# Recurrence of a hybrid decoder layer: an own tile for the off-diagonal blocks, other operand roles for the sample queries, other PSUM banks, and part of the elementwise work on another engine

## Chip, core and metric

The kernel runs on one core of a Trainium2 chip. A core has TensorE (PE, with its weight loads as PEld), VectorE (DVE), ScalarE (ACT), GpSimd (POOL) and the queue engine SyncE (SP), all with their own instruction streams that wait for one another by semaphores. The metric is the device time of one launch in microseconds; lower is better.

## What is computed

The launch runs two layers of a decoder trunk in float32, for a prompt of 512 tokens and 8 samples of 8 tokens, 576 columns in all. Each layer has a pooling mixer, a gated linear recurrence (HGRN2), latent attention, their merge, and a gated feed-forward part. The change touches the recurrence and, through the engine that prepares it, the pooling mixer. Per head (4 heads, key and value size 128) the recurrence is:

```python
def step(S, blk):
    qc, kc, vc, lc = blk
    L = jnp.cumsum(lc, axis=2)
    inter = jnp.einsum('bhtk,bhkv->bhtv', qc * jnp.exp(L), S)
    diff = jnp.where(causal, L[:, :, :, None, :] - L[:, :, None, :, :], -jnp.inf)
    A = jnp.einsum('bhtk,bhsk,bhtsk->bhts', qc, kc, jnp.exp(diff))
    intra = jnp.einsum('bhts,bhsv->bhtv', A, vc)
    L_end = L[:, :, -1:, :]
    S = jnp.exp(L_end[:, :, 0, :, None]) * S + jnp.einsum('bhsk,bhsv->bhkv', kc * jnp.exp(L_end - L), vc)
    return S, inter + intra
```

The pooling mixer has 4 groups of 128 channels with windows 2, 4, 8 and 16; a group's mean minus the token goes through a 128x128 matrix.

## The kernel before

Tokens lie along the free dimension, channels along the 128 partitions. Every engine's order is written out by hand; there is no scheduler. A layer runs: input projections, attention, sample attention, then the stretch of this study, then the merge quads, output, feed-forward.

**The stretch before the recurrence.** PE projects the pooling input (four tiles `TILE_U`), the gate (four tiles `TILE_HGATE`) and then the four pooling products (`TILE_YPOOL`), which wait for `pool_d_ready`. Meanwhile POOL works out, for heads 0 and 1, the exponents of seven levels (`level_differences`, line 646) and of the ends (`ends_differences`, line 665), ACT takes their exponentials (`decays_levels`, `decays_ends`), and POOL multiplies by the queries (`level_scaled`, line 657, and `ends_scaled`). DVE does the pooling mixer.

**The recurrence.** There are 20 steps `n`: for each head, 4 chunks of 128 prompt tokens and one sample step (`c == 4`) of 64 columns. PE runs `hg_pair_scores(n+1)` ahead of `hg_sums(n)`. A pair part has 28 matmuls of 32-column weights (lines 1044, 1048 and 1053: diagonal blocks in an even bank, off-diagonal ones in an odd bank) and a transposition of the keys (line 1058) into bank 6. DVE masks and sums the levels and writes the diagonal blocks into `scores_hg` (lines 2235, 2238, 2244: `pair_sums`); ACT copies the keys out of bank 6 and then, behind `hg_scores`, three off-diagonal blocks into the same `scores_hg` (line 1558, `hg_full`). The sums part has scores times values (line 1068), queries times state (line 1073) and keys times values (line 1078), after which DVE updates the state (line 2261: `update`). In a sample step PE multiplies the 8 states as weights of 128 columns by 8 query columns each (line 1090) and the keys by the values laid out in 8 blocks, two matmuls of 512 columns over 64 partitions (line 1098), into bank 7 and into the odd bank of that step; DVE then updates 8 states (line 2273). The pair part two steps on writes that odd bank and waits for `hg_state`.

**Heads 2 and 3** are prepared inside the recurrence: POOL takes the differences and `ends_scaled`; ACT takes the exponentials at the steps that `LEVEL_STEPS` and `END_STEPS` name (step: head, first level, end); DVE does `level_scaled` behind steps 4 and 13. POOL's differences of head 3 come behind `ends_scaled` of head 2, and its buffers are free when head 0's or head 1's sample step is done (`hg_upd`). After the last step PE sums squares (line 880 from `lq`, `ones`) and starts the merge.

## Time and profile before

| | us |
|---|---|
| median of 3 runs (lowest, highest) | 2368.7 (2366.51, 2369.54) |
| the profiled execution, its span | 2366.31, 2364.5 |
| PE busy in the span | 2258.8 (96%) |
| DVE, ACT, POOL busy | 1167.7, 507.0, 1085.3 |
| recurrence, first layer (first pair matmul to first square sum) | 324.98 to 398.85 |
| recurrence, second layer (first pair matmul) | from 1497.02 |

The span is the profiled time between the first and the last instruction; 1.8 us of the execution lie around it. The granted clock is the share of TensorE's full 2.4 GHz that it was given; 0.50 is 1.2 GHz.

### The profile page before, as it was taken

How to read it: one execution, taken by the hardware profiler on the slowest of the kernel's cores; microseconds unless marked ns; L12 is line 12 of the kernel's file. 1: busy time of each engine (PE TensorE's matmuls, PEld its weight loads, DVE VectorE, ACT ScalarE, POOL GpSimd, SP SyncE). 2: the span in 40 equal slices, each digit the busy share in tenths (PEclk: the TensorE clock that was granted, in tenths of full speed). 3: DMA queues.
4: the chain of work that ended last, by engine and by line, in shares of the span. 5: the costliest groups of instructions: out<-in, count | busy, mean ns of one | idle time of the engine just before them, and what ended most of it. 6: DMA issues, size and time to landing. Idle time of an engine off the chain costs nothing.

```text
span 2364.5 us, 36665 instructions
## 1 busy us (share of the span) xinstructions
PE 2258.8 (96%) x11752; PEld 1734.4 (73%) x11752; DVE 1167.7 (49%) x1983; ACT 507.0 (21%) x1066; POOL 1085.3 (46%) x1260
## 2 busy tenths in 40 slices
PE   8999888999998999999899989889999899999997
PEld 6775676777776777777676757667777677777775
DVE  0534464432466666671216345553325766666612
ACT  1434334111112001000124333331111211001002
POOL 0000545666664676633300007446666646676342
PEclk9999997999999999999999999879999999999998
DMA  5221121222212222222032221222221312222211
GB/s 205 91 81 49 56 77 65 81 80 73 72 68 107 71 82 78 71 81 74 36 128 85 72 62 41 78 73 73 81 81 63 120 57 86 71 79 75 81 62 40
DMA packets 51612, 183.42 MB, mean 78 GB/s; under 512 B 7234, under 2 KB 27970, under 8 KB 37762
## 3 DMA queue, kind: packets, MB, share of 16 engines
q1 hardware_dynamic: 50882, 178.49, 22.0%
q10 hardware_dynamic: 576, 3.00, 0.3%
q8 instruction: 82, 1.34, 0.2%
q14 instruction: 72, 0.59, 0.1%
HBM read 172.28 MB, written 9.18 MB: 77 GB/s over the span
## 4 chain that ended last, share of the span: by engine, by line
PE 86%; DVE 4%; SPq 4%; issue 3%; POOL 1%; ACT 1%; DMA 0%; DVEq 0%; ACTq 0%; POOLq 0%
PE ps L1177 24%; PE ps L1105 19%; PE ps L1215 16%; PE ps L880 14%; PE ps L1453 3%; PE ps L1380 2%; PE ps L901 2%; SPq L717 1%; SPq L729 1%; PE ps L1245 1%; SPq L722 1%; PE ps L912 1%; PE ps L1098 1%; DVE xT L2006 1%; PE ps L1367 1%
## 5 line engine op out<-in xcount | busy, mean ns | idle before, releaser
L880 PE MATMUL ps<-xT,wring 128*128 128x288 f32 (+2 forms) x1152 | 280.5, 406 | 1.4 <-DVE o_mla L2176 1.4
L880 PEld LDWEIGHTS ps<-xT,wring 128*128 128x128 f32 x1152 | 218.7, 190 | 62.0 <-issue 1.7
L1177 PE MATMUL ps<-lq,mreg 128*128 128x288 f32 x1008 | 251.3, 406 | 0.0
L1177 PEld LDWEIGHTS ps<-lq,mreg 128*128 128x128 f32 x1008 | 191.5, 190 | 52.9
L1558 ACT ACTIVATE r<-ps 128x288 f32<-128x288 f32 (+7 forms) x268 | 113.1, 428 | 537.1 <-PE ps L1105 251.7
L1177 PE MATMUL ps<-xT,wring 128*128 128x288 f32 x672 | 169.8, 406 | 0.0
L1177 PEld LDWEIGHTS ps<-xT,wring 128*128 128x128 f32 x672 | 127.7, 190 | 35.3
L1105 PE MATMUL ps<-r,kbuf 128*128 128x288 f32 x576 | 143.6, 406 | 0.0
L2636 POOL TENSOR_TENSOR kbuf<-o_mla 128x288 f32<-128x288 f32 x42 | 33.3, 794 | 221.9 <-DVE o_mla L2406 221.9
L653 POOL TENSOR_TENSOR side<-lq 128x256 f32<-128x256 f32 x20 | 13.0, 652 | 258.7 <-PE ps L1481 258.7
L1105 PEld LDWEIGHTS ps<-r,kbuf 128*128 128x128 f32 x576 | 109.4, 190 | 30.2
L2663 POOL TENSOR_TENSOR kbuf<-kbuf,lq 128x2304 f32<-128x2304 f32 x2 | 10.1, 5049 | 257.3 <-DVE side L2113 257.3
L1851 ACT ACTIVATE r<-r 128x592 f32<-128x592 f32 x44 | 30.7, 697 | 428.0 <-DVE r L2443 427.8
L1558 ACT ACTIVATE o_mla<-ps 128x288 f32<-128x288 f32 (+1 forms) x108 | 45.5, 421 | 338.4 <-PE ps L1215 214.5
L2443 DVE SCALAR_TENSOR_TENSOR r<-r,small 128x592 f32<-128x592 f32 x88 | 104.6, 1189 | 12.4 <-DVE r L2440 12.1
L2440 DVE SCALAR_TENSOR_TENSOR r<-r,small 128x592 f32<-128x592 f32 x88 | 104.5, 1188 | 12.4 <-DVE r L2437 11.4
L1105 PE MATMUL ps<-xT,wring 128*128 128x288 f32 x384 | 97.2, 407 | 1.8 <-ACT lq L1580 1.8
L1215 PE MATMUL ps<-r,side 128*128 128x288 f32 x372 | 92.7, 407 | 0.8 <-DVE r L2454 0.8
L1105 PEld LDWEIGHTS ps<-xT,wring 128*128 128x128 f32 x384 | 72.8, 190 | 22.7 <-issue 2.7
L1177 PE MATMUL ps<-xT,mreg 128*128 128x288 f32 x336 | 88.3, 406 | 0.0
L1177 PE MATMUL ps<-lq,wring 128*128 128x288 f32 x336 | 88.3, 406 | 0.0
L1105 PE MATMUL ps<-lq,r 128*128 128x288 f32 x336 | 87.6, 407 | 0.7 <-DVE side L2324 0.7
(412 smaller groups left out, 4595.9 us busy)
## 6 DMA issues: line engine op xcount, KB each, us to landing
wring<-w_stream SPq DMA_DIRECT2D x100, 1024.0 KB, 4.9
side<-w_stream SPq DMA_DIRECT2D x18, 704.0 KB, 4.3
r<-pages_in SPq DMA_DIRECT2D x80, 128.0 KB, 2.1
vbuf<-w_stream SPq DMA_DIRECT2D x12, 512.0 KB, 3.7
r<-w_stream SPq DMA_DIRECT2D x12, 512.0 KB, 3.6
wring<-w_stream SPq DMA_DIRECT2D x8, 704.0 KB, 4.2
r<-w_stream SPq DMA_DIRECT2D x6, 704.0 KB, 4.2
mreg<-pages_in SPq DMA_DIRECT2D x32, 128.0 KB, 2.1
```

Source lines behind the costliest of these rows:

```text
L880: mm = pe.matmul(out[0:w.shape[-1], a * 512:a * 512 + hi - lo], w, x[:, lo:hi], start=(k == 0), stop=(k == len(pairs) - 1))
L901: mm = pe.matmul(slot(tile + j)[:, a * 512:a * 512 + hi - lo], w, xT[:, k, lo:hi], start=(k == 0), stop=(k == KD - 1))
L1105: mm = pe.matmul(banks[name], ws[:, k * P:(k + 1) * P], xs[:, k, :], start=(k == 0), stop=(k == n - 1))
L1177: mm = pe.matmul(up_sum[name], ws[:, k * P:(k + 1) * P], xs[:, k, :], start=(k == 0), stop=(k == HK - 1))
L1215: mm = pe.matmul(res_bank(which, m, i - 1), ws[:, k * P:(k + 1) * P], x, start=(k == 0), stop=(k == len(xs) - 1))
L1380: mm = pe.matmul(bank[2 * x + a][:, 0:HALF], w, xT[:, k, a * HALF:(a + 1) * HALF], start=(k == 0), stop=(k == KD - 1))
L1453: mm = pe.matmul(slot(TILE_HI + m)[0:rows, part * 256:(part + 1) * 256], xT[:, k, m * P:m * P + rows], w_slot[part][:, k * 256:(k + 1) * 256],
L1558: return act.activation(out, in_, func, **more)
L1851: act.activation(conv_h[u][0][:, 0:CX - 2], conv_h[u][0][:, 0:CX - 2], ACT.Silu).then_inc(silu_done.sem, 1)
L2440: dve.scalar_tensor_tensor(out=out, in0=src[:, 1:CX - 1], scalar=scalar(col + 2 * KF), in1=out, op0=ALU.mult, op1=ALU.add).then_inc(conv_s ...
L2443: dve.scalar_tensor_tensor(out=out, in0=src[:, 2:CX], scalar=scalar(col + 4 * KF), in1=out, op0=ALU.mult, op1=ALU.add).then_inc(conv_done. ...
L2636: pool.tensor_tensor(up_v[u], up_u2[u], up_p5s[u], ALU.add).then_inc(up_v_ready.sem, 1)
```

## The change

It does six things. (1) The off-diagonal blocks get a tile of their own, `off_hg`, zeroed once; ACT fills it as soon as the pair part is there, before the keys, and PE multiplies it by the values in a matmul of its own, ahead of the one with `scores_hg`. (2) In a sample step a 32-column window of queries is the weight and the state of each sample the moving operand; the rows go through `s_rows` and come back by two matmuls with a selecting matrix `pick`. (3) The keys times values of samples are two matmuls over 32 partitions each, in banks 7 and 6; the transposed keys move into the odd bank of the step. Waits of the pair part go. (4) DVE prepares heads 0 and 1 instead of POOL. (5) The pooling groups run in the order 3, 2, 1, 0. (6) `LEVEL_STEPS`, `END_STEPS` and the multiplication steps move.

```diff
-LEVEL_STEPS = {0: (2, 0, 2), 1: (2, 2, 5), 2: (2, 5, 7), 10: (3, 0, 2), 11: (3, 2, 5), 12: (3, 5, 7)}
-END_STEPS = {7: 2, 13: 3}
+LEVEL_STEPS = {3: (2, 0, 3), 5: (2, 3, 7), 10: (3, 0, 3), 11: (3, 3, 7)}
+END_STEPS = {7: 2, 12: 3}
+MULT_STEPS = {7: 2, 13: 3}
+GROUP_OF = (3, 2, 1, 0)
...
-            return bank[7] if part == 0 else bank[2 * (n % 2) + 1]
+            return bank[7 - part]
+
+        def turned_bank(n):
+
+            return bank[2 * (n % 2) + 1][:, P:2 * P]
...
-                if n >= 2 and (n - 2) % (N_CHUNK + 1) == N_CHUNK:
-
-                    pe.wait_ge(*hg_state.at(l, ((n - 2) // (N_CHUNK + 1) + 1) * (N_CHUNK + 2)))
-                if c == N_CHUNK:
-                    pe.wait_ge(*hg_k_rows.at(l, n))
...
-                if 1 <= n and c < N_CHUNK:
-                    pe.wait_ge(*hg_k_rows.at(l, n))
-                pe.transpose(bank[6][0:w, 0:P], decayed[:, h % 2, 1, t0:t0 + w], ident).then_inc(hg_turned.sem, 1)
+                pe.transpose(turned_bank(n)[0:w, :], decayed[:, h % 2, 1, t0:t0 + w], ident).then_inc(hg_turned.sem, 1)
...
-                    mm = pe.matmul(bank[4][:, t0:t1], v_hg[:, c, h * P:(h + 1) * P], scores_hg[:, n % 2, :],
-                                   start=True, stop=(c == 0))
+                    pe.matmul(bank[4][:, t0:t1], v, off_hg[:, n % 2, :], start=True, stop=False)
+                    pe.wait_ge(*hg_scores.at(l, n + 1))
+                    mm = pe.matmul(bank[4][:, t0:t1], v, scores_hg[:, n % 2, :], start=False, stop=(c == 0))
...
+                for b in range(DEC_BATCH):
+                    x, j = divmod(b, S_PAIRS)
+                    t0 = SEQ + min(DEC_SEQ * b, SAMPLES - SUB)
+                    mm = pe.matmul(bank[5][SUB * j:SUB * (j + 1), 256 + x * P:256 + (x + 1) * P],
+                                   decayed[:, h % 2, 0, t0:t0 + SUB], state_s[:, b, h, :], start=True, stop=True)
+                mm.then_inc(s_rows_made.sem, 1)
+                pe.wait_ge(*hg_k_rows.at(l, n + 1))
+                pe.wait_ge(*blocks_ready.at(l, h + 1))
+                pe.wait_ge(*hg_state.at(l, ups))
+                for part in range(2):
+                    rows = slice(SUB * part, SUB * (part + 1))
+                    pe.matmul(upd_bank(n, part), k_rows[rows, n % 2, :], v_blocks[rows, :, :],
+                              start=True, stop=True).then_inc(hg_upd.sem, 1)
+                pe.wait_ge(*hg_scores.at(l, n + 1))
+                pe.wait_ge(*hg_o_taken.at(l, 3 * h + 2))
...
+                for x in range(2):
+                    mm = pe.matmul(bank[5][:, 0:SAMPLES], s_rows[:, x * P:(x + 1) * P], pick[x], start=False,
+                                   stop=(x == 1))
...
-                pe.wait_ge(*taken_at(l, TILE_YPOOL + 1))
+                pe.wait_ge(*taken_at(l, TILE_YPOOL + 3))
...
+                def ready_head(h):
+                    dve.wait_ge(*lev_exp.at(l, h + 1))
+                    level_scaled(dve, h)
+                    dve.wait_ge(*ends_exp.at(l, h + 1))
+                    dve.tensor_tensor(decayed[:, h % 2, 0, :], decayed[:, h % 2, 0, :], q_hg[:, h, :], ALU.mult
+                                      ).then_inc(lev_ready.sem, 1)
+
+                dve.wait_ge(*smp_cols_taken.at(l, S_PAIRS))
+                dve.wait_ge(*log_k_ready.at(l, 1))
+                for h in range(2):
+                    level_differences(dve, h).then_inc(lev_diff.sem, 1)
+                    ends_differences(dve, h).then_inc(lev_diff.sem, 1)
...
+                    if i in (0, 2):
+                        ready_head(i // 2)
...
-                        dve.wait_ge(*hg_o.at(l, 2 * h + 2))
-                        dve.tensor_copy(q_hg[:, h, SEQ:T], bank[5][:, 0:SAMPLES]).then_inc(hg_o_taken.sem, 1)
+                        dve.wait_ge(*s_rows_made.at(l, h + 1))
+                        dve.tensor_copy(s_rows, bank[5][:, 256:512]).then_inc(hg_o_taken.sem, 1)
```

On PE, at the first sample step (step 4, behind the pair part of step 5), the program before has:

```order
L1058 MATMUL ps<-const,mreg 128x128 [waits hg_k_rows]
L1086 MATMUL ps<-mreg,vbuf 128x64 [waits state_s_ready,hg_scores]
L1090 MATMUL ps<-mreg,r 128x8 x8
L1097 REGISTER_ALU [waits blocks_ready,hg_k_rows]
L1098 MATMUL ps<-mreg 128x512 [waits hg_state]
L1098 MATMUL ps<-mreg 128x512
L1031 REGISTER_ALU [waits hg_scores]
L1044 MATMUL ps<-lq,r 32x32 [waits hg_state]
```

The changed program has at the same place:

```order
L1062 MATMUL ps<-const,mreg 128x128
L1093 MATMUL ps<-r1,mreg 32x128 [waits state_s_ready]
L1093 MATMUL ps<-r1,mreg 32x128 x7
L1096 REGISTER_ALU
L1098 REGISTER_ALU [waits blocks_ready,hg_k_rows]
L1101 MATMUL ps<-mreg 128x512 [waits hg_state]
L1101 MATMUL ps<-mreg 128x512
L1104 ISA [waits hg_scores]
L1105 MATMUL ps<-mreg,vbuf 128x64 [waits hg_o_taken]
L1108 MATMUL ps<-const,r2 128x64 x2
L1050 MATMUL ps<-lq,r1 32x32 [waits hg_scores]
```

The scores matmul moved behind the state updates and now waits for DVE's copy of the rows; the wait of the next pair part for DVE's state updates is gone.

On PE, in a chunk step, the changed program has one matmul more (L1073 with `off_hg`), and the wait for the scores stands behind it:

```order
L1062 MATMUL ps<-const,mreg 128x128
L1073 MATMUL ps<-off_hg,vbuf 128x128 [waits hg_full]
L1074 REGISTER_ALU
L1075 MATMUL ps<-mreg,vbuf 128x128 [waits hg_scores]
L1077 REGISTER_ALU
L1079 MATMUL ps<-mreg,side 128x128 [waits hg_state]
L1084 MATMUL ps<-vbuf,mreg 128x128 [waits hg_k_rows]
```

On DVE, ahead of the pooling mixer (the last instructions of head 1's differences, then the first sums of pooling group 3), the changed program has:

```order
L665 TENSOR_TENSOR r<-kbuf,lq 128x4x64
L678 TENSOR_TENSOR r<-kbuf,lq 128x576
L680 TENSOR_TENSOR mreg<-lq,kbuf 128x64
L2213 REGISTER_ALU
L2219 TENSOR_TENSOR r<-r 128x710 [waits tile_act]
```

Behind that group come head 0's multiplications:

```order
L2230 SCALAR_TENSOR_TENSOR r<-r 128x496
L2236 SCALAR_TENSOR_TENSOR r<-r 128x64
L2239 COPY r<-r 128x15
L2240 COPY r<-r 128x120
L673 TENSOR_TENSOR side<-side,lq 128x256 [waits lev_exp]
L673 TENSOR_TENSOR mreg<-mreg,lq 128x32
```

Before, DVE went from the copies of the history (L2183) straight to the first group's sums (L2196); the differences and multiplications of both heads stood on POOL.

## Rows read from the trace of the kernel before

**Rows 1.** The page, busy time by engine.
```profile
PE 2258.8 (96%) x11752; PEld 1734.4 (73%) x11752; DVE 1167.7 (49%) x1983; ACT 507.0 (21%) x1066; POOL 1085.3 (46%) x1260
```

**Rows 2.** Windows over both recurrences: engines busy, granted clock, DMA share, GB/s.
```profile
324.98:398.85 73.87, 58.06 (x1158) 44.78 (x1157) 44.60 (x137) 31.09 (x103) 35.79 (x37) 0.78 0.17 63
1497.02:1572.00 74.98, 61.65 (x1158) 46.83 (x1158) 44.65 (x137) 31.33 (x103) 36.83 (x37) 0.72 0.16 62
```

**Rows 3.** Timeline, PE, sample step of head 0 at the full clock: start, us.
```profile
335.92 0.27 PE L1044 MATMUL ps<-lq,r 128*32 128x32 f32 x8
336.87 0.43 PE L1086 MATMUL ps<-mreg,vbuf 64*128 64x64 f32 x2
337.23 1.95 PE L1090 MATMUL ps<-mreg,r 128*128 128x8 f32 x16
339.12 1.98 PE L1098 MATMUL ps<-mreg 64*128 64x512 f32 x4
343.07 0.34 PE L1044 MATMUL ps<-lq,r 128*32 128x32 f32 x8 [1.98 <-DVE r L2273]
```

**Rows 4.** Timeline, PE, the sums of a chunk at the full clock.
```profile
390.15 0.39 PE L1068 MATMUL ps<-mreg,vbuf 128*128 128x128 f32 x2
390.37 0.39 PE L1073 MATMUL ps<-mreg,side 128*128 128x128 f32 x2
390.91 0.26 PE L1044 MATMUL ps<-lq,r 128*32 128x32 f32 x4
```

**Rows 5.** Timeline, PE, head 3 at 1.2 GHz, then the square sums.
```profile
374.89 0.69 PE L1086 MATMUL ps<-mreg,vbuf 64*128 64x64 f32 x2
379.02 3.78 PE L1098 MATMUL ps<-mreg 64*128 64x512 f32 x4
386.37 0.34 PE L1044 MATMUL ps<-lq,r 128*32 128x32 f32 x8
389.16 0.34 PE L1044 MATMUL ps<-lq,r 128*32 128x32 f32 x8
398.85 6.29 PE L880 MATMUL ps<-lq,ones 128*128 128x288 f32 x16 [1.22 <-DVE r L2273]
```

**Rows 6.** Timeline, PE, matmuls over 32 partitions in the sample attention.
```profile
219.49 1.09 PE L970 MATMUL ps<-r,side 32*64 32x512 f32 x8
```

**Rows 7.** Timeline, DVE, level sums of a chunk and state updates of samples.
```profile
332.33 0.36 DVE L2235 TENSOR_TENSOR r<-ps,const 128x192 f32<-128x192 f32 x1 [0.35 <-PE ps L1053]
333.26 0.29 DVE L2244 TENSOR_TENSOR mreg<-ps,const 128x128 f32<-128x128 f32 x1
357.18 2.16 DVE L2273 SCALAR_TENSOR_TENSOR r<-r,end_decay,ps 128x128 f32<-128x128 f32 x8 [0.83 <-PE ps L1098]
```

**Rows 8.** Timeline, the preparation of head 3 on ACT and POOL.
```profile
348.43 0.68 ACT L1759 ACTIVATE r<-r 128x576 f32<-128x576 f32 x1
352.43 0.61 POOL L653 TENSOR_TENSOR side<-lq 128x256 f32<-128x256 f32 x1
362.59 1.41 POOL L667 TENSOR_TENSOR r<-kbuf,lq 128x576 f32<-128x576 f32 x1
369.27 0.68 ACT L1759 ACTIVATE r<-r 128x576 f32<-128x576 f32 x1
373.39 0.34 PE L1044 MATMUL ps<-lq,r 128*32 128x32 f32 x8 [3.07 <-POOL mreg L2530]
```

**Rows 9.** Timeline, the stretch ahead: pooling on DVE, the products on PE.
```profile
276.03 6.61 DVE L2196 TENSOR_TENSOR r<-r 128x710 f32<-128x710 f32 x1 [15.04 <-ACT r L1558]
309.20 0.21 DVE L2217 COPY r<-r 128x120 f32<-128x120 f32 x1
320.99 4.06 PE L880 MATMUL ps<-r,small 128*128 128x288 f32 x16
```

**Rows 10.** Timeline, DVE, multiplications of a head's levels.
```profile
369.34 0.42 DVE L662 TENSOR_TENSOR side<-side,lq 128x256 f32<-128x256 f32 x1
369.68 0.18 DVE L662 TENSOR_TENSOR mreg<-mreg,lq 128x32 f32<-128x32 f32 x1
```

134 lines of the change are left out of this document (60 added, 74 removed).

## The prediction

> **What bounds the kernel now.** I read the page by engine first: PE is busy 96% of the span [rows 1]. A change elsewhere is worth something only where PE waits, or runs slowly. The windows over the recurrences show both [rows 2]: in the first, 73.87 us long, PE is busy 58.06 us, so it waits 15.8; in the second, 74.98 us to its end mark, 61.65. And the granted clock is 0.78 and 0.72, a mixture of 2.4 and 1.2 GHz with some 44% and 56% of the time at the lower. No other engine is near full there (DVE 44.6 us). The timeline then shows what ends PE's waits. Behind the sample step of head 0, PE stands 1.98 us until DVE has updated the sample states [rows 3]; before head 3 it stands 3.07 us for POOL's last product [rows 8].
>
> **A chunk step on PE.** At the full clock pairs and transposition take 336.87 - 335.92 = 0.95 us [rows 3] and the sums 390.91 - 390.15 = 0.76, so 1.71 together; one matmul of the sums is 390.37 - 390.15 = 0.22 [rows 4]. The change adds one (`off_hg` times values): 1.93. At 1.2 GHz the same step is 389.16 - 386.37 = 2.79 [rows 5], and the added matmul 0.43 (twice 0.22): 3.22. So on 16 chunk steps a layer the edit costs PE 3.5 us at the full and 6.9 at the half clock. What it buys: the sums part need not wait for ACT's copies behind the scores. DVE's chain from mask to scores is 333.26 + 0.29 - 332.33 = 1.22 us [rows 7], and it lies beside 1.93 us of PE; then nothing on the path waits for ACT in a plain step.
>
> **A sample step on PE.** Now, from the start of the 64x64 matmul to the end of the updates: 339.12 + 1.98 - 336.87 = 4.23 us at the full clock [rows 3], and 379.02 + 3.78 - 374.89 = 7.91 at the half [rows 5]. After it:
> - 8 matmuls with 32-column weights and 128 moving columns, 16 passes. A pass of 128 columns is 0.11 us (half of the 0.22 [rows 4]). Four column groups side by side, as the pair parts use them, give 16 x 0.11 / 4 = 0.44; two side by side 0.88; one after the other 1.76. I take 0.44, since 48 passes of pair work and a transposition fit into 0.95 us [rows 3].
> - two updates of 512 columns over 32 partitions, in two banks. One after the other they cost today's 1.98 us [rows 3]; side by side half. The nearest row is the sample attention's, 8 passes of 512 columns over 32 partitions in 1.09 us [rows 6], where one by one they would need 8 x 1.98 / 4 = 3.96. I take 1.0.
> - scores and two selecting matmuls of 64 columns, with two new full weight loads: 0.5.
>
> Sum 1.95 us at the full clock, 3.8 at the half: 2.3 to 4.1 us less for each of 8 sample steps, and 1.3 to 3.2 even if nothing runs side by side in the updates.
>
> **The wait behind it** changes place. The next pair part starts at once, but the next head's first update writes bank 7 and waits for DVE's 8 state updates (2.16 us [rows 7]), which now have a copy of 256 columns, some 0.4 us, ahead. PE has 0.5 + 0.95 + 0.66 us of other work for this, so I leave 0.6 us of waiting where 1.98 stood [rows 3]. Queued behind that waiting matmul is all of PE; DVE waits in turn only for that update.
>
> **The stretch before.** The pair part now waits for all four pooling products to be taken: +0.9 us. DVE gets, for each of two heads, 14 large and 6 small differences, two more for the ends, and 7 + 3 + 1 products. With 0.34 us for a large (369.68 - 369.34) and 0.18 for a small one [rows 10], and 0.7 for one of 576 columns: some 6.9 and 4.0 us a head. The 13.8 us of differences fill the 15.04 us in which DVE waits for ACT [rows 9]; the 8.0 of products lie ahead of the pooling's end, which is 309.20 + 0.21 = 309.4, while PE first needs it at 320.99 [rows 9]. 11.6 us of cover, so this costs nothing; without the cover it would cost up to 8 a layer. The other order of groups is hidden by the same cover. POOL, freed, begins head 2's differences earlier, which hides them deeper.
>
> **The first seven steps.** I count PE's work until the transposition of step 7 is ready and ACT can begin head 2's end exponentials: seven pair parts of 0.95, one sample pair of 0.6, four sums 3.9, one sample step 1.95, two sums 2.0, waits 0.9, the late start 0.9, ACT's copies 0.65. That is 16.9 + 0.6 from 324.98, so 342.5; before it was 348.43 [rows 8]. **5.9 us**.
>
> **From there to head 3** another chain sets the time: ACT's ends of head 2, POOL's product, POOL's differences of head 3 (362.59 - 352.43 = 10.2 us), ACT's exponentials and ends, POOL's product. It took 373.39 - 348.43 = 25.0 us [rows 8]. The change touches one link: exponentials in two pieces instead of three and the ends a step earlier, 5.6 by the same rows instead of 369.27 - 362.59 = 6.7 [rows 8]. PE would be through its five to six steps sooner, so it waits: here part of the gain is given back as waits for ACT, on the first sums of head 2. Head 3 begins at 342.5 + 23.9 = 366.4, **7.0 us** earlier in all.
>
> **Head 3** took 398.85 - 373.39 = 25.5 us [rows 5, 8], much of it at 1.2 GHz. After, at the full clock: five pair parts 4.4, two sample steps 3.9, sums 3.8, and waits 3.0 (last one: 2.16 of updates and a copy behind the selecting matmuls): 15.1. All at the half clock: 27.2. Before, the clock fell behind waits and behind 8-column matmuls and rose during dense chunk steps. The 8-column matmuls go, the wait before head 3 stays. I take the middle, 21.1: **4.4 us**. The square sums behind it take 6.29 us, mostly at 1.2 GHz [rows 5]; 16 such matmuls take 4.06 at the full clock [rows 9]. Half of the 2.2 between, **1.1 us**.
>
> The Trainium skill, "TensorE: Matmul & The Clock Gate" (Part 1: The HAM clock gate), says that the throttled state is the default and activity releases it. By that rule the denser sample step would keep the clock up, and head 3 would come nearer 15.1 than 21.1. The rows agree so far as dense steps stand before each rise; they don't say which head will be how dense.
>
> **Sum.** 7.0 + 4.4 + 1.1 = 12.5 us a layer, and 25 for two. The profiled execution took 2366.3 (span 2364.5 and 1.8 around it); the median of the three runs lies 2.4 above it. 2366.3 - 25 = 2341, and with part of that distance I say **2342 us**.
>
> **Rivals.**
> - *The clock stays up.* Without 8-column matmuls no stretch may be sparse enough. Then head 3 is 15.1 and the square sums 4.1: 7.0 + 10.4 + 2.2 = 19.6 a layer, 2327 to 2329. Against it: PE waits 3 us and more for ACT in head 2, and the clock fell behind less.
> - *Head 3 stays at 1.2 GHz and heads 0 and 1 lose clock as before.* Head 3 27.2, 2.5 us lost ahead of it: 7.0 - 2.5 - 1.7 = 2.8 a layer, 2361. For it: the added matmul costs most here, and the wait ahead of head 3 is still there.
> - *Slower: the lower clock throughout the recurrence.* Place: all 20 steps. 16 x 3.22 + 4 sample pairs of 1.1 + 4 x 3.8 + 5.3 of waits = 76.4 against 73.9 and 74.4: +4.5 for two layers, 2371. It decides when more than about nine tenths of PE's work is at 1.2 GHz, against 44% and 56% of the time now.
> - *DVE late for the pooling products.* Its added 21.8 us would have to cost more than about 33 to use up the cover. Operations of 256 columns at twice the 0.34 would cost some 10 us a layer on the path: 2361 again.
> - *Row tiles don't run side by side.* +1.0 x 8 at most, of which waits hide some: 2347. It lies in the forecast's own range.
>
> The Trainium skill, "TensorEngine Tiling (Array Packing)" (Tiling Modes, Key Properties), says that changing the tiling mode drains TensorE. That speaks against the sample step, which now goes through one or two more modes. No row isolates a drain; the pair-to-transposition change lies inside the 0.95 us above. The sum would rise by little, and no chance changes.
>
> **Numbers.** Forecast (2335 to 2352) 0.58, clock up 0.14, clock low in head 3 or DVE late 0.20, slower 0.05, no effect at all 0.03. To leave out no more than 2 in 10 the range goes from 2328 to 2359. This kernel's measurement can tell about 0.2%, or 4.7 us: faster 0.92, same 0.03, slower 0.05.
>
> **What would show it.** Sample steps of about 2 us at the full clock, the eight state matmuls in under 0.5, the two updates in about 1.0. No wait of the pair matmuls for DVE; instead the keys-times-values matmul of a head's first chunk waits for it. PE waits for ACT's copies in head 2's chunks, in all more than before. POOL's head 3 differences end near 356. The pooling products start at 321 as now. Wrong: if the first recurrence is over 68 us, look at the clock by head first; if it is under 56, at whether the chain over POOL bound at all.

## The result: 16 us faster, and the profile after

The changed kernel takes **2352.05 us** (median of 4 runs, 2350.25 to 2355.85) against 2368.12 for the kernel before in the same comparison (4 runs, 2366.51 to 2369.54). The ratio is 0.9934, with a 95% interval of 0.9917 to 0.9952: 16 us less, 12 to 20 by the interval. The forecast was 2342, with a range of 2328 to 2359. The profiled execution took 2352.96, its span is 2351.1. The page by engine, as in [rows 1]:

```profile
PE 2240.8 (95%) x11848; PEld 1719.8 (73%) x11848; DVE 1171.9 (50%) x2124; ACT 505.5 (21%) x1066; POOL 995.4 (42%) x1128
```

The windows over the two recurrences, from the first pair matmul to the first square sum, and over head 3 of the first layer (columns as in [rows 2]: length, busy time of the engines, granted clock, DMA share, GB/s):

```profile
329.19:392.13 62.94, 46.55 (x1205) 36.98 (x1205) 45.11 (x140) 28.45 (x102) 33.47 (x37) 0.95 0.20 74
1492.93:1559.33 66.40, 53.59 (x1205) 41.55 (x1205) 44.59 (x140) 28.57 (x102) 34.49 (x37) 0.82 0.19 70
374.86:392.13 17.27, 14.60 (x328) 11.22 (x328) 13.83 (x45) 4.08 (x19) 14.19 (x9) 0.90 0.01 2
```

The first recurrence went from 73.87 to 62.94 us. The second, which ended at 1571.38 before (1571.38 - 1497.02 = 74.36), went to 66.40. That is 10.9 and 8.0 us. Up to that same mark the second window of the kernel before reads:

```profile
1497.02:1571.38 74.36, 61.03 (x1158) 46.33 (x1157) 44.65 (x137) 31.33 (x103) 36.21 (x37) 0.72 0.17 62
```

All of this gain is in TensorE's busy time, which fell by 11.5 and 7.4 us (58.06 to 46.55, 61.03 to 53.59); part of that is less work, part the higher granted clock. TensorE is still busy only 46.55 of 62.94 us in the first, so 16.4 us of waiting are left, about as much as the 15.8 before, though the waits that I had read there are gone. The timeline of TensorE names the new ones; the steps in between are left out:

```profile
333.85 0.42 PE L1050 MATMUL ps<-side 128*32 128x32 f32 x26
336.45 0.29 PE L1050 MATMUL ps<-side 128*32 128x32 f32 x11 [2.19 <-issue]
...
340.42 0.63 PE L1093 MATMUL ps<-r,mreg 128*32 128x128 f32 x12
342.49 0.41 PE L1093 MATMUL ps<-r,mreg 128*32 128x128 f32 x4 [1.44 <-issue]
...
366.05 0.80 PE L1073 MATMUL ps<-off_hg,vbuf 128*128 128x128 f32 x2 [5.22 <-ACT off_hg L1568]
...
374.86 0.24 PE L1050 MATMUL ps<-lq,r 128*32 128x32 f32 x5 [1.31 <-issue]
```

Two things stand out. In the pair part of step 3, and inside the sample step of head 0, TensorE stops in the middle of a row of like matmuls (after 26 of 37, after 12 of 16) for 2.19 and 1.44 us, and the profile names no releaser. Layer 1 has the same two stops, at the same instructions, with 2.68 and 1.71 us. And at step 11 it waits 5.22 us for ScalarE's copy into `off_hg`. In layer 1, where TensorE came to these steps more slowly, that wait is spread over steps 10, 11 and 12 (1.43, 0.90 and 1.58 us). The stop at 374.86 is put down to issue as well, but it has a plain cause: VectorE's products of head 3, which this pair part waits for, end at 374.75 (its row is below).

The sample step of head 3, as in [rows 3], and the square sums, as in [rows 5]:

```profile
387.44 0.65 PE L1093 MATMUL ps<-r,mreg 128*32 128x128 f32 x16
388.44 1.13 PE L1101 MATMUL ps<-mreg 32*128 32x512 f32 x4 [0.36 <-DVE side L2286]
389.50 0.43 PE L1105 MATMUL ps<-mreg,vbuf 64*128 64x64 f32 x2
389.86 0.66 PE L1108 MATMUL ps<-const,r 128*128 128x64 f32 x4
392.13 5.81 PE L891 MATMUL ps<-lq,ones 128*128 128x288 f32 x16 [1.61 <-DVE lq L2304]
```

The states' 16 passes take 0.65 us (1.95 before), the updates 1.13 (1.98). The pair matmuls behind a sample step start at once, where they stood 1.98 us for VectorE [rows 3].

### The profile page after: what moved, and what is told of

It is laid out like the page before. It is cut to its first block, busy times and chain, and to the rows that moved or that the text cites. A ratio compares the mean times of both kernels' runs of the same rounds, so it can differ in the third digit from the quotient of the medians.

```text
span 2351.1 us, 36952 instructions
## 1 busy us (share of the span) xinstructions
PE 2240.8 (95%) x11848; PEld 1719.8 (73%) x11848; DVE 1171.9 (50%) x2124; ACT 505.5 (21%) x1066; POOL 995.4 (42%) x1128
## 4 chain that ended last, share of the span: by engine, by line
PE 86%; SPq 4%; DVE 4%; issue 3%; POOL 1%; ACT 1%; DMA 0%; DVEq 0%; ACTq 0%; POOLq 0%
PE ps L1188 24%; PE ps L1116 19%; PE ps L1226 16%; PE ps L891 14%; PE ps L1464 3%; PE ps L1391 2%; PE ps L912 2%; SPq L728 1%; SPq L740 1%; PE ps L1256 1%; SPq L733 1%; PE ps L923 1%; PE ps L1050 1%; DVE xT L2016 1%; PE ps L1378 1%
## 5 line engine op out<-in xcount | busy, mean ns | idle before, releaser
L2558 POOL TENSOR_TENSOR mreg<-vbuf,const 64x512 f32<-64x512 f32 x8 | 8.3, 1033 | 272.2 <-PE ps L1492 263.0
L2467 DVE SCALAR_TENSOR_TENSOR r<-r,small 128x592 f32<-128x592 f32 x88 | 104.6, 1189 | 12.4 <-DVE r L2464 10.9
```

Of the source, the lines that this page charges most:

```text
L2467: dve.scalar_tensor_tensor(out=out, in0=src[:, 1:CX - 1], scalar=scalar(col + 2 * KF), in1=out, op0=ALU.mult, op1=ALU.add).then_inc(conv_s ...
```

## Experiments

Every kernel was timed in turn with the kernel before on one chip; the medians of the kernel before in these comparisons lie between 2368.1 and 2369.8 us, and a step n means the same as above (steps 0 to 4 are head 0, 5 to 9 head 1, 10 to 14 head 2, 15 to 19 head 3). The columns are the median, its ratio to the kernel before with the 95% interval, and for the two layers of the profiled execution the length of the recurrence and the clock granted in it.

| kernel | us | ratio | layer 0 | layer 1 |
|---|---|---|---|---|
| before | 2368.1 | | 73.9 (0.78) | 74.4 (0.72) |
| changed | 2352.05 | 0.9934 (0.9917, 0.9952) | 62.9 (0.95) | 66.4 (0.82) |
| e1_loads_late | 2347.3 | 0.9914 (0.9901, 0.9927) | 62.8 (0.86) | 62.8 (0.84) |
| e2_loads_mid | 2353.2 | 0.9941 (0.9928, 0.9954) | 66.7 (0.85) | 64.5 (0.79) |
| e3_levels_first | 2360.1 | 0.9968 (0.9958, 0.9977) | 69.6 (0.85) | 69.4 (0.83) |
| e4_off_after_sums | 2352.95 | 0.9931 (0.9919, 0.9943) | 66.7 (0.85) | 68.0 (0.77) |
| e5_same_rows | 2357.6 | 0.9959 (0.9944, 0.9974) | 69.2 (0.78) | 69.6 (0.78) |
| e6_queries_moving | 2361.9 | 0.9971 (0.9959, 0.9983) | 71.1 (0.73) | 68.3 (0.82) |
| e7_gpsimd_prepares | 2353.0 | 0.9934 (0.9917, 0.9950) | 63.4 (0.95) | 62.8 (0.95) |
| e8_before_loads_late | 2368.3 | 0.9996 (0.9988, 1.0005) | 73.7 (0.75) | 74.5 (0.75) |
| e9_states_held | 2361.1 | 0.9965 (0.9954, 0.9976) | 69.8 (0.78) | 69.9 (0.80) |
| c1_split_differences | 2349.1 | 0.9918 (0.9904, 0.9931) | 64.7 (0.79) | 62.8 (0.81) |
| c2_port_in_turn | **2331.95** | 0.9847 (0.9834, 0.9859) | 54.3 (0.93) | 53.3 (0.97) |
| c3_in_turn_off_waits | 2329.9 | 0.9844 (0.9829, 0.9859) | 55.6 (1.00) | 55.4 (1.00) |

How far one profile can be trusted shows in e7_gpsimd_prepares: in the recurrence TensorE has the same instructions as in the changed kernel, and its second recurrence took 62.8 us at a granted clock of 0.95 where the changed kernel's took 66.4 at 0.82. A single recurrence is known to some 4 us. The intervals are 2 to 4 us wide on either side, so two kernels whose medians lie closer than that are not told apart.

### What the new stops are

The theory: they are TensorE's own instructions coming late. The trace has packets of 16 KB on an instruction queue (q8); it doesn't say for which engine. In the DMA view of the changed kernel for 334 to 335 us and for 340 to 340.5, one such packet moves inside the bulk transfers that are issued at 329 to 331 (2 MB of sample states, 0.27 MB of `pool_o`, twice 1 MB of `wring`):

```profile
q1 hardware_dynamic: 18, 0.29, 91.4%
q8 instruction: 1, 0.02, 6.0%
...
q1 hardware_dynamic: 29, 0.22, 104.8%
q8 instruction: 1, 0.02, 12.4%
```

TensorE stops at 334.3 and goes on at 336.45; it stops at 341.05 and goes on at 342.49. Later packets, with no transfer beside them (345 to 350, 350 to 355), have no stop. The packet itself takes about 1 us of one DMA engine in either case (6.0% of a microsecond of 16 engines here, 6.3% at 347), so if instructions come late, the time is lost around the packet and not in it. The rival: the stops belong to these places of the program. Two kernels move the transfers, with the same edit in SyncE's program, once with step 12 and once with step 5 as the mark.

```diff
+                sp.wait_ge(*hg_pairs.at(l, 13))
                 sp.dma_start(pool_out[bass.ds(l, 1)].rearrange("o p g n c -> (o p) g n c"), pool_last
                              ).then_inc(mixer_stored.sem, 16)
                 load(l, MERGE0)
                 load(l, MERGE0 + 1)
```

> The changed kernel with three transfers of the recurrence (the store of pool_o and the first two 1 MB loads of wring) held back until the pair part of step 12 is done; only the 2 MB load of the sample states stays where it was. Theory (the new idle times of TensorE put down to issue, 2.19 us at 336.45 and 1.44 us at 342.49 in layer 0, 2.68 and 1.71 in layer 1, are TensorE's own instructions arriving late, because a 16 KB packet of the instruction queue stands in line with the bulk transfers): the gap inside the sample step of head 0 is gone in both layers (1.4 + 1.7 = 3.1 us), the one in the pair part of step 3, which lies inside the load of the states, stays; about 2349 us. If the loads now meet another instruction packet, near step 13 to 16, a gap of 1 to 2 us shows up there instead and the time stays at 2352. Rival (the gaps belong to the place in the program, whatever the transfers do): both gaps stay, 2352 us.

> The same three transfers held back only until the pair part of step 5 is done, some 345 us into the execution. In the changed kernel an instruction packet moves between 345 and 350 and again between 350 and 355 with no transfer beside it and no gap on TensorE. Theory (instructions arrive late behind bulk transfers): the gap at 342.5 is gone, and a gap put down to issue of 1 to 2.5 us appears in steps 5 to 9 of head 1, where there was none; about 2352 us. Rival (gaps belong to the place in the program): the gaps stay where they were and none appears in head 1; 2352 us. The two differ in where the gaps are, not in the time.

TensorE's timeline of e1_loads_late, steps 3 and 4:

```profile
332.62 0.29 PE L1051 MATMUL ps<-side 128*32 128x32 f32 x11 [2.21 <-issue]
...
336.59 0.65 PE L1094 MATMUL ps<-r,mreg 128*32 128x128 f32 x16
```

The 16 passes of the states now run through in both layers; the stop in step 3 is where it was, under the load of the states. And of e2_loads_mid, in head 1 of layer 0, with the DMA view of 345 to 346 us:

```profile
347.46 0.22 PE L1051 MATMUL ps<-r 128*32 128x32 f32 x1 [2.32 <-issue]
```

```profile
q1 hardware_dynamic: 61, 0.39, 95.5%
q8 instruction: 1, 0.02, 6.0%
```

A stop of 2.32 us appeared in a pair part of head 1, where there had been none, with an instruction packet among the moved loads (at 345.3) 2 us ahead of its end. In layer 1 none appeared, and the time stayed. There the moved loads ran from 1508 to 1516, between two packets: the one at 1507.5 came ahead of them and the one at 1515.75 when they filled only 10% of the engines. So no packet met them in that layer, and both layers fit the theory. The third kernel holds the load of the states back too, until the pair part of step 3 is done.

```diff
                 sp.wait_ge(*taken_at(l, TILE_YPOOL + 3))
+                sp.wait_ge(*hg_pairs.at(l, 4))
                 sp.dma_start(state_s.rearrange("p b h v -> p (b h v)"),
```

> e1_loads_late with the 2 MB load of the sample states held back as well, until the pair part of step 3 is done, so that nothing bulky moves in the first three steps. Theory (the gap of 2.2 us in the pair part of step 3 is the same as the other: instructions behind the states' transfer): that gap is gone in both layers or falls under 0.7 us; in return the sample step of head 0 waits for the states, which land 9 us after their issue: 3.5 to 5.5 us; about 2350 to 2354 us. Rival (the gap at step 3 belongs to the place in the program): it stays at 1.8 us or more.

```profile
331.74 0.27 PE L1052 MATMUL ps<-lq,r 128*32 128x32 f32 x8
331.83 0.51 PE L1052 MATMUL ps<-side 128*32 128x32 f32 x38
...
340.86 1.08 PE L1095 MATMUL ps<-r,mreg 128*32 128x128 f32 x16 [4.76 <-DMA r<-hgrn_state]
```

The pair part of step 3 runs through, in both layers, and in its place stands the forecast wait for the states, 4.76 and 4.55 us. The packets at 333.0 and 1503.5 come about half a microsecond ahead of the load here, and no stop follows them. So each of the two stops goes when its transfer goes, and one came where a transfer was put: that bulk transfers cause the stops is shown. That what comes late is TensorE's instructions is inferred from the packets beside each stop. The time (2361) is 7 us above the expected range: besides the wait for the states, both recurrences ran at a clock of 0.78 and 0.80, for 0.86 and 0.84 in e1_loads_late; why they did is open. The Trainium skill, "Runtime: NRT & Kernel Launch" (Instruction fetch mechanics), says that instructions come in blocks of 16 KB over a queue of their own, and that the cost of a block's end is mostly hidden. The packets of 16 KB agree; where bulk transfers fill the engines, 1.4 to 2.7 us a block were not hidden here.

> The kernel before with the same three transfers held back until the pair part of step 12. Its trace has no gap put down to issue in either recurrence, though its instruction packets at 334 to 336 and 338 to 340 move inside the same transfers. Theory (TensorE ran slowly enough there, at half the clock for long stretches and with waits of 3 us in the first five steps, that its instructions came in time behind the transfers): no change, 2366 to 2371 us, so the 5 us that holding back gives the changed kernel were a cost that the change had brought. Rival (the transfers slow something else of the recurrence, the PSUM or SBUF side, in both kernels): 2364 us or less.

The kernel before gains nothing from the same edit (0.9996). One packet a layer moves well inside the transfers there (at 335.1 and 1508.3; the one at 338.75 comes when they are nearly over, at 9% of the engines), and no stop follows. So a packet among bulk transfers is not enough for a stop. The likely reason is the pace: behind the packet at 335.1 stands the old sample step, in which TensorE needed only 22 matmul records for the 4.2 us from 336.87 to 341.10 [rows 3]. No run tests this by itself.

What it is worth in time: 2347.3 against 2352.05, 4.7 us, in line with 3.1 us of stops, but the intervals of the two ratios overlap (0.9917 to 0.9927 lies in both), and layer 0's recurrence stayed at 62.8, at a lower granted clock (0.86 for 0.95). The gain in time is likely, not shown.

### What holds head 3 back

The wait of 5.22 us at step 11 has a chain behind it that the changed kernel's rows on GpSimd and ScalarE show. GpSimd waits 4.33 us for head 2's exponentials, takes their product, and only then makes head 3's differences; ScalarE stands 7.29 us for these with TensorE's copies queued behind:

```profile
351.08 2.26 POOL L2553 TENSOR_TENSOR mreg<-mreg,lq 128x576 f32<-128x576 f32 x1 [4.33 <-ACT mreg L1775]
353.30 0.61 POOL L664 TENSOR_TENSOR side<-lq 128x256 f32<-128x256 f32 x1
...
363.56 1.48 ACT L1759 ACTIVATE side<-side 128x1536 f32<-128x1536 f32 x1 [7.29 <-POOL mreg L665]
```

The first try changes the order of two calls.

```diff
                 value_blocks(l, 1)
-                ends_scaled(l, 2)
                 differences(l, 3)
+                ends_scaled(l, 2)
```

> The changed kernel with two calls on GpSimd changed in order: the level differences of head 3 ahead of the product that ends head 2's preparation. In the changed kernel GpSimd sits idle 4.33 us for ScalarE ahead of that product (351.08) and finishes head 3's differences at 363.5, while ScalarE sits idle 7.29 us for them and TensorE 5.22 us (366.05) for ScalarE's copies queued behind. Theory (this chain is what kept head 3 from its forecast start): the 5.22 us wait goes to under 1, about 0.4 us comes at the first pair part of head 2, ScalarE's exps of steps 11 and 12 leave 1 to 3 us of waits; net 3 to 4 us for each layer, about 2345 us. Rival (GpSimd is the bound of the recurrence in any order, and head 2's product is then late): the wait moves to the first pair part of head 2 with 3 us or more, 2351 to 2355 us.

It went the wrong way, to 2360.1, by neither mechanism. GpSimd was through with the differences at 358.5, 5 us earlier, and the wait for ScalarE at step 11 was gone. But TensorE waited 9.49 us (8.66 in layer 1) for VectorE's scores. VectorE's and GpSimd's timelines of that kernel:

```profile
350.61 1.05 DVE L673 TENSOR_TENSOR r<-r,lq 128x256 f32<-128x256 f32 x1
353.57 6.36 DVE L673 TENSOR_TENSOR mreg<-mreg,lq 128x32 f32<-128x32 f32 x1
359.85 1.86 DVE L673 TENSOR_TENSOR r<-r,lq 128x256 f32<-128x256 f32 x6
```

```profile
353.12 0.25 POOL L664 TENSOR_TENSOR mreg<-lq 128x32 f32<-128x32 f32 x1
...
358.49 1.39 POOL L2553 TENSOR_TENSOR mreg<-mreg,lq 128x576 f32<-128x576 f32 x1
```

A product of 128x32, which takes 0.18 us [rows 10], stood 6.36 us, to 359.93; GpSimd's row of back-to-back operations ended at 358.49 + 1.39 = 359.88. The three products ahead of it got in between GpSimd's operations, at 0.93 to 1.21 us each (the first is shown). Those of VectorE's operations that read PSUM kept their times beside GpSimd (0.36, 0.50 and 0.29 us at 349.1 to 350.3 there). The Trainium skill, "SBUF — State Buffer" (Who interferes with whom), has this: a VectorE instruction with two SBUF inputs contends with a GpSimd instruction that reads SBUF, and the second to come is blocked for the whole of the other. The trace agrees on which instructions meet. It differs in how long: the fourth product waited out not one GpSimd instruction but some ten. Why it did and the first three did not is open. The changed kernel had paid a little of it, at 372.03 (1.39 us for another 128x32), and its next products end at the 374.75 that released head 3:

```profile
372.03 1.39 DVE L673 TENSOR_TENSOR mreg<-mreg,lq 128x32 f32<-128x32 f32 x1
...
374.01 0.74 DVE L673 TENSOR_TENSOR mreg<-mreg,lq 128x256 f32<-128x256 f32 x2
```

So the two engines' instructions with two SBUF inputs are best laid out in turn, like users of one resource. Two kernels try that, both with the loads late. The first:

```diff
-LEVEL_STEPS = {3: (2, 0, 3), 5: (2, 3, 7), 10: (3, 0, 3), 11: (3, 3, 7)}
+LEVEL_STEPS = {3: (2, 0, 3), 5: (2, 3, 7), 9: (3, 0, 3), 10: (3, 3, 7)}
-MULT_STEPS = {7: 2, 13: 3}
+MULT_STEPS = {8: 2, 13: 3}
...
+                pool.wait_ge(*hg_pairs.at(l, N_CHUNK + 1))
+                level_differences(pool, 3, 0, 4)
                 pool.wait_ge(*hg_upd.at(l, N_CHUNK + 2))
                 ends(l, 2)
                 value_blocks(l, 1)
+                level_differences(pool, 3, 4).then_inc(lev_diff.sem, 1)
                 ends_scaled(l, 2)
-                differences(l, 3)
```

> The changed kernel with the transfers held back as in e1_loads_late, and GpSimd's differences for head 3 in two pieces: levels 0 to 3 as soon as the pair part of step 4 is done (head 0's level buffer is free then, 338.4 in the changed kernel) and not 4.33 us idle later, levels 4 to 6 behind head 2's ends, the product of head 2's preparation last; VectorE's seven products of head 2 one step later (8, not 7), and ScalarE's exps of head 3 in steps 9 and 10 (10 and 11 before). What e3_levels_first showed is kept out of the way: there one of VectorE's products (128x32, both inputs in SBUF) stood 6.36 us beside a row of GpSimd's operations, and ended with the row. Theory (the chain GpSimd to ScalarE is what keeps head 3 late, and the products wait only while GpSimd works): GpSimd is through with head 3's differences about 10 us earlier than at 363.5, the wait of 4 to 5 us at step 11 goes, 0.5 to 1.5 us comes back for the products in step 8 and for ScalarE's exps; 3 to 4 us in layer 0 and 2 to 3 in layer 1 below e1_loads_late's 2347: about 2341 us. Rival (VectorE's products meet GpSimd again and hold the sums): waits of 3 us or more in steps 8 and 9, 2347 to 2355 us.

```profile
347.42 3.57 DVE L673 TENSOR_TENSOR r<-r,lq 128x256 f32<-128x256 f32 x1
```

```profile
349.30 1.40 POOL L2554 TENSOR_TENSOR mreg<-mreg,lq 128x576 f32<-128x576 f32 x1
```

```profile
353.36 0.34 PE L1051 MATMUL ps<-lq,r 128*32 128x32 f32 x8 [4.15 <-DVE r L673]
```

The rival came out: the differences are done at 349.3, the wait at step 11 is gone, and VectorE's first product stood 3.57 us until GpSimd's last operation had ended (350.70; the product at 350.99). TensorE waited 4.15 us in each layer for it, and 2.3 and 2.1 us more ahead of head 3, and the time is that of e1_loads_late, within the error. The second kernel puts one wait between them, and moves the products of head 3 from step 13 to step 12:

```diff
-MULT_STEPS = {8: 2, 13: 3}
+MULT_STEPS = {7: 2, 12: 3}
...
                 value_blocks(l, 1)
+                pool.wait_ge(*late_ready.at(l, 1))
+                ends_scaled(l, 2)
                 level_differences(pool, 3, 4).then_inc(lev_diff.sem, 1)
-                ends_scaled(l, 2)
```

ScalarE's first exponentials of head 3 (levels 0 to 2) no longer wait for the end of the differences there, since these levels are in the first piece.

> The changed kernel with the transfers held back as in e1_loads_late and GpSimd's and VectorE's use of two SBUF inputs put in turn: GpSimd makes head 3's levels 0 to 3 right behind the pair part of step 4, then head 2's ends and value blocks, waits for VectorE's products of head 2 (step 7 again, 2.7 us), and only then does head 2's product and levels 4 to 6. ScalarE's exps of head 3 in steps 9 and 10, VectorE's products of head 3 in step 12 (13 before). In c1_split_differences a single product (128x256) took 3.57 us until GpSimd's row ended and TensorE waited 4.15 us for it. Theory (VectorE's instructions with two SBUF inputs stand still while GpSimd has work, and nothing else of the recurrence is left between 4 and 12): no product of head 2 above 0.5 us each, no wait of 4 us or more in steps 7 to 11 of layer 0 (e1_loads_late had 4.17 there), about 1 us of waits behind each set of products; recurrences of 58 to 61 us against 62.8 in e1_loads_late, 2339 to 2344 us. Rival (the sum of what VectorE, GpSimd and ScalarE have to do for the two late heads sets the time, the wait goes elsewhere in each order): recurrences of 62 to 64 us again and 2347 to 2350.

```profile
347.24 1.85 DVE L673 TENSOR_TENSOR r<-r,lq 128x256 f32<-128x256 f32 x6
```

```profile
349.26 1.41 POOL L2554 TENSOR_TENSOR mreg<-mreg,lq 128x576 f32<-128x576 f32 x1 [2.76 <-DVE r L673]
```

```profile
327.99:382.28 54.29, 46.66 (x1205) 36.82 (x1205) 44.04 (x140) 28.70 (x102) 31.74 (x35) 0.93 0.24 86
1481.83:1535.10 53.27, 45.28 (x1204) 35.58 (x1205) 43.85 (x140) 28.58 (x102) 31.98 (x36) 0.97 0.25 87
```

**2331.95 us**, 38 below the kernel before and 20 below the changed one: the products run at 0.31 us a piece, GpSimd waits 2.76 us for them, and in each layer one stop of 2.1 us (step 3, under the states) and no wait of over 2 us is left. This beats both kernels. It lies 7 us below the expected range: with head 3's products out of GpSimd's way its pair part has no wait either, and the clock was higher than in e1_loads_late (0.93 and 0.97 for 0.86 and 0.84).

How much of this is the order? Against c1_split_differences the two recurrences of the profiles are 10.4 and 9.5 us shorter. TensorE's waits shrank by 4.1 and 3.5 of that; the other 6.3 and 6.0 are busy time of the same instructions at a higher granted clock (0.93 and 0.97 for 0.79 and 0.81). That the two rose together is seen in this pair of runs, not explained. And c2 differs from c1 in three things, the wait, the earlier products and ScalarE's wait that went; none was tried alone.

### What each part of the change brought

Four kernels undo one part each in the changed kernel, and a fifth undoes the first of these parts in c2_port_in_turn. First the own tile: ScalarE waits again for the sums.

```diff
                     if c < N_CHUNK:
+                        act.wait_ge(*hg_scores.at(l, n + 1))
                         full, off = off_hg[:, n % 2, :], bank[2 * (n % 2) + 1]
```

> The changed kernel with one part undone: ScalarE waits again for VectorE's summed block (hg_scores) of a chunk before it copies the off-diagonal blocks, though they go to their own tile. Nothing is left out. VectorE needs about 1.2 us from the end of a pair part to the summed block and ScalarE 0.78 us behind it, 2.0 us, where TensorE is back at the sums of that chunk after some 1.9 us at the full clock. Theory (the own tile takes a wait away that matters only at the full clock): 0.1 to 0.5 us for each of the 16 chunk steps of a layer that run at the full clock, 2 to 6 us for each layer less what lies under ScalarE's and VectorE's other waits; 2355 to 2362 us. Rival (the wait is hidden, and the gain of the change came from the sample steps and the earlier preparation alone): 2351 to 2354 us.

> c2_port_in_turn with the edit of e4_off_after_sums on top: ScalarE again waits for VectorE's summed block before it copies the off-diagonal blocks to their own tile. In the changed kernel that wait moved nothing (2352.95 against 2352.05), though both its recurrences looked longer in the profile (66.7 and 68.0 us against 62.9 and 66.4). Theory (the own tile takes away a wait that stands in every chunk step, and was covered in the changed kernel by the chain of head 3; in c2_port_in_turn, 54.3 and 53.3 us, that chain is gone and the steps run at the full clock at 1.7 to 1.9 us): 0.1 to 0.3 us for each of 32 chunk steps and 1 us where ScalarE's exps stand behind it, 3 to 10 us in all, 2335 to 2342 us. Rival (the copies are early enough with the wait too, and the own tile brings nothing in either): 2330 to 2334 us.

2352.95 and 2329.9: nothing, in both settings. The windows over the recurrences of c3_in_turn_off_waits, under those of c2_port_in_turn above:

```profile
328.92:384.54 55.62, 44.31 (x1205) 34.63 (x1205) 44.56 (x140) 28.89 (x102) 31.57 (x36) 1.00 0.24 84
1483.24:1538.64 55.40, 44.31 (x1204) 34.63 (x1205) 44.58 (x140) 28.98 (x102) 31.70 (x36) 1.00 0.24 84
```

With the wait back, TensorE stands 7.0 us for ScalarE's copies into `off_hg` in layer 0, where it stood 1.0, twice 2.5 us of it beside VectorE's products. But it had the full clock throughout and was busy 44.31 us, not 46.66. The recurrences are only 1.3 and 2.1 us longer, and the medians differ by 2 the other way, within the error. Waits and clock went opposite ways here; what ties them is left open.

Next the updates in two row groups, of which the second takes the same rows as the first (this leaves the states of four samples wrong):

```diff
-                    rows = slice(SUB * part, SUB * (part + 1))
+                    rows = slice(0, SUB)
```

> The changed kernel in which the second of the two state updates of a sample step takes the same 32 rows of weights and values as the first (so the states of four of the eight samples come out from the wrong rows; the instructions are the same in number and size). Theory of the forecast (the two updates run side by side because they use different rows of the array, four passes in 1.13 us where one pass of 512 columns alone takes 0.21 us of columns at 2.4 GHz and two updates one behind the other 1.7): 0.7 us more in each of 8 sample steps, of which the next pair part follows at once, 4 to 6 us in all, 2355 to 2358 us. Rival (they are one behind the other already, or the time is hidden behind VectorE's updates): 2351 to 2353 us.

The four passes of the updates in the sample step of head 0, at the full clock, and of head 2, at half:

```profile
340.18 1.98 PE L1101 MATMUL ps<-mreg 32*128 32x512 f32 x4
377.18 3.78 PE L1101 MATMUL ps<-mreg 32*128 32x512 f32 x4
```

And the same passes in different rows at half the clock, in head 2 of layer 1 of the changed kernel:

```profile
1542.55 2.08 PE L1101 MATMUL ps<-mreg 32*128 32x512 f32 x4
```

1.98 us against 1.13 at the full clock, 3.78 against 2.08 at half: the updates do run side by side in different rows and not in the same. The time is 5.5 us longer, as expected, but the intervals of the two ratios overlap (0.9944 to 0.9952 lies in both).

The next kernel puts the old product of the states back:

```diff
-                for b in range(DEC_BATCH):
-                    x, j = divmod(b, S_PAIRS)
-                    t0 = SEQ + min(DEC_SEQ * b, SAMPLES - SUB)
-                    mm = pe.matmul(bank[5][SUB * j:SUB * (j + 1), 256 + x * P:256 + (x + 1) * P],
-                                   decayed[:, h % 2, 0, t0:t0 + SUB], state_s[:, b, h, :], start=True, stop=True)
...
+                for b in range(DEC_BATCH):
+                    t0 = SEQ + b * DEC_SEQ
+                    mm = pe.matmul(bank[5][:, b * DEC_SEQ:(b + 1) * DEC_SEQ], state_s[:, b, h, :],
+                                   decayed[:, h % 2, 0, t0:t0 + DEC_SEQ], start=False, stop=(b == DEC_BATCH - 1))
```

> The changed kernel with the product of states and sample queries put back as it was (eight products with a 128-column state as weights and 8 moving columns, added to the scores' product ahead of the updates; no s_rows and no picks); the updates stay in their two row groups and banks. Nothing is left out. Theory (this edit and the updates made the sample step 2.3 us shorter at the full clock and 4 at half): by the rows of before the products of the eight samples took some 1.9 us and the new way 1.0 (0.44 and half a microsecond of picks), and the wait for VectorE's scores comes back ahead of the updates, in all 1.5 to 2.5 us for each of 8 sample steps, more where the clock is low; 2363 to 2372 us. Rival (the sample step's length lies behind VectorE's and ScalarE's work in all but one or two steps): 2352 to 2358 us.

```profile
355.84 1.99 PE L1095 MATMUL ps<-mreg,r 128*128 128x8 f32 x16
```

2361.9, 1 us below the expected range: 9.9 us for the queries as weights. On TensorE at the full clock it is 1.99 us of states and 0.4 of scores against 0.65 and 0.95. That is 0.8 us for each of 8 sample steps, 6 in all. The rest goes with the granted clock, 0.73 and 0.82 for 0.95 and 0.82, and with a longer last wait for VectorE's updates (2.2 us ahead of the square sums for 1.6).

The last part is the preparation of heads 0 and 1, given back to GpSimd:

```diff
-                for h in range(2):
-                    level_differences(dve, h).then_inc(lev_diff.sem, 1)
-                    ends_differences(dve, h).then_inc(lev_diff.sem, 1)
...
+                differences(l, 0)
+                ends(l, 0)
+                differences(l, 1)
+                ends(l, 1)
+                scaled(l, 0)
+                ends_scaled(l, 0)
                 value_blocks(l, 0)
+                scaled(l, 1)
+                ends_scaled(l, 1)
```

> The changed kernel with heads 0 and 1 prepared by GpSimd again (differences, ends and both products), VectorE having only the pooling; the order of ScalarE's exps and of the groups stays that of the changed kernel. Nothing is left out. Theory (this edit costs and brings nothing by itself: GpSimd was through with both heads at 304.5 in the kernel before and idle for 4.75 us and 21.7 us behind it, so head 2's differences are no later): 2350 to 2354 us. Rival (VectorE's pooling windows, which have both inputs in SBUF, stand still beside GpSimd's operations as its products did in e3_levels_first, and the pooling products come late): the first pair part starts 3 us or more later in its layer, 2357 us or more.

2353.0: the edit is worth nothing that the intervals could tell, as forecast. VectorE's cover held (in the changed kernel the pooling products wait for nothing of it), and GpSimd had nothing better to do.

So undoing the states' product costs some 10 us and undoing the row groups of the updates some 5.5, the latter within overlapping intervals; undoing the other two parts costs nothing. These are costs of single parts in the changed kernel, and it is chance that they add up to its 16 us. The other banks were not undone in any run, and with them the waits that the pair part lost: in the kernel before TensorE stood for VectorE behind a sample step (1.98 us [rows 3]), and in the steps of head 0 for ScalarE's copies of the keys, which had to leave bank 6:

```profile
330.28 0.33 PE L1058 MATMUL ps<-const,mreg 128*128 128x128 f32 x1 [1.26 <-ACT mreg L1558]
334.65 0.26 PE L1044 MATMUL ps<-lq,r 128*32 128x32 f32 x4 [0.89 <-ACT mreg L1558]
```

All of these are gone in the changed kernel. What that is worth in time stays open, and so does the order of ScalarE's exponentials and of the pooling groups, which was not tried alone either.

## The prediction, point by point

The forecast said faster, by 25 us, and it was 16. Its steps:

- **The chunk step** was forecast at 1.93 us at the full clock; the transpositions of steps 7 and 8 are 349.21 - 347.31 = 1.90 us apart. Right. That nothing on the path waits for ScalarE in a plain step was right too, but what the own tile was said to buy was nothing, by e4 and c3.
- **The sample step** was forecast at 1.95. The states take 0.6 (0.44 forecast), the updates 1.06 (1.0), but the scores and the two selecting matmuls 0.36 + 0.59 = 0.95 (0.5): 2.6 in all. This term was 0.65 us too small, 2.6 us a layer. The rival in which row tiles don't run side by side is excluded by e5.
- **The wait behind it**, 0.6 in place of 1.98: there is none behind the sample step; 0.4 to 0.6 us stand ahead of its own updates or scores. Right in size; I had put them ahead of the next head's first update.
- **The stretch before** was costed at nothing and 0.9 of a later start. The 0.91 us is there in every profile of the changed kernel and its variants, and the cover held: TensorE has no wait in its projections up to the last pooling product. That layer 0 began at 329.19 and not 325.9 is, as far as the traces tell, not the change: the long row of projections ahead of it already began 3.2 us later (262.04 for 258.81), and the profiles of the twelve other kernels begin the recurrence between 325.3 and 330.8.
- **The first seven steps.** Counted from the first pair part, ScalarE should have begun head 2's ends after 16.6 us (23.45 before); it began them after 348.45 - 329.19 = 19.3. The two stops of 2.19 and 1.44 are more than the 2.7 us missing; without them the rest would have been about a microsecond early. In layer 1 it took 21.2 us, with stops of 2.68 and 1.71. I had not foreseen that TensorE's own instructions could come late; that the stops go with the bulk transfers is shown by e1 and e9, and by e2 where a packet met them.
- **From there to head 3**: 23.9 forecast, 374.86 - 348.45 = 26.4 measured (24.96 before). This step failed. I had kept the chain's rows and left out that ScalarE would stand in front of it with TensorE's copies queued behind, which made a wait of 5.22 us where I had "waits for ACT, on the first sums of head 2", and that VectorE's products stand beside GpSimd's (1.39 us for 0.18), which released head 3. With the first it should have been a term of the sum; the second was in no step. GpSimd's differences of head 3, forecast to end near 356, ended at 363.50. Head 3 began 45.7 us behind the first pair part and not 40.5 (47.1 in layer 1).
- **Head 3**: 21.1 forecast, 17.3 in layer 0 and 19.3 in layer 1, at granted clocks of 0.90 and 0.74, between the two cases that I had set (15.1 and 27.2). The middle was 2 to 4 us too long. The square sums took 5.81 in both layers, 0.5 and 1.3 less, for the 1.1.
- **The sum**, for the recurrences alone: 12.3 us a layer forecast, 10.9 and 8.0 measured. The direction and the mechanism of the sample step were right; the mis-sized terms are the way to head 3 (5.2 us short) and head 3 itself (2 to 4 the other way). That these two errors pull against each other is luck, and keeps the total nearer to the forecast than its parts. The profiles also hold a loss that was in no term: the recurrences and square sums gave 18.9 + 1.8 = 20.7 us, but the two profiled executions differ by only 13.4 (2366.31 - 2352.96), since the first recurrence began 4.2 us later and the stretch from its square sums to the second one grew by 3.1. The waits of 0.91 are a part of both, and 3.2 of the 4.2 had gathered ahead of the projections; the rest is open. The medians differ by 16.
- **The rivals.** The clock did rise, as "the clock stays up" had it, to 0.95 in layer 0, and yet the time of that rival did not come, since the stops and the chain took its place: a faster TensorE ran into other bounds. "Head 3 stays at 1.2 GHz", "slower" and "DVE late" did not come either (0.90 and 0.74 in head 3, no wait for the pooling products). Which clock a layer gets differs between executions of the same TensorE instructions (0.82 and 0.95).

## To carry to other kernels

When a change makes one engine faster, look at what its trace shows as free only because the engine was slow: here most likely its instructions, which came in time behind bulk transfers at the old pace. Loads that are not needed yet can be issued when nothing dense runs. And before moving work between VectorE and GpSimd, list the instructions with two SBUF inputs on both and lay them out in turn, with a wait if need be: the same work took 2349 us where the two met (c1) and 2332 in turn (c2). In the profiles the larger part of that is TensorE's busy time at a higher granted clock, the smaller part its waits.

## What the hardware showed

- In the changed kernel each instruction packet of 16 KB that moved inside bulk transfers (91% and more of the DMA engines) went with a stop of TensorE of 1.4 to 2.7 us; packets without them, or just ahead of them, went with none. In the kernel before such a packet (335.1) went with none either.
- A VectorE operation with two SBUF inputs beside GpSimd's back-to-back operations got in between them after 0.9 to 1.2 us in three cases; in two others (3.57 and 6.36 us, the latter for 0.18 us of work) it was done only at the end of the row. Operations that read PSUM kept their times.
- Two updates of 512 columns over 32 rows each took 1.13 us in different rows and 1.98 in the same at the full clock, 2.08 and 3.78 at half.
- Of 7 us of waits for ScalarE in c3 against 1 in c2, 1.3 to 2.1 us were left in the recurrence, at a clock of 1.00 against 0.93 and 0.97.
